# Two-layer decoder trunk on one core: merged router operations, another order at the entry of the expert loops, residual scaled tile by tile, down conversions in the last pass, last norm on three engines

## The reference

```python
h = layer_norm(ALPHA * h + mix, ln_g[layer, 0], ln_b[layer, 0])
ffn = grouped_moe(h, router_w, router_bias, moe_w_gate[layer], moe_w_up[layer], moe_w_down[layer])
h = layer_norm(ALPHA * h + ffn, ln_g[layer, 1], ln_b[layer, 1])

def grouped_moe(x, router_w, router_bias, w_gate, w_up, w_down):
    scores = jax.nn.softmax((xt @ router_w).astype(jnp.float32), axis=-1)
    ...      # best of 4 groups by the sum of its top 2, then the top 2 experts inside it
    h = jax.nn.silu(jnp.einsum('td,edf->tef', xt, w_gate)) * jnp.einsum('td,edf->tef', xt, w_up)
    h = h * gates[..., None].astype(h.dtype)
    y = jnp.einsum('tef,efd->td', h, w_down)
```

## Time and profile before

| what | us |
|---|---|
| median of 3 runs | 1335.28 |
| lowest and highest run | 1328.35 and 1341.85 |
| the profiled execution's own time | 1329.78 |
| its span, first to last instruction | 1328.1 |
| PE busy | 1180.5 (89%) |
| DVE busy | 909.9 (69%) |
| ACT busy | 685.1 (52%) |
| POOL busy | 184.9 (14%) |
| mean DMA rate | 213 GB/s |

### The profile page before, as it was taken

One profiled execution on the slowest core, in us unless ns is written; L12 is line 12 of the kernel. 1 busy time (PEld: TensorE's weight loads), 2 busy tenths in 40 slices (PEclk: granted clock), 3 DMA queues, 4 the chain that ended last, 5 costly groups with the idle time before them and its releaser, 6 DMA issues.

```text
span 1328.1 us, 14735 instructions
## 1 busy us (share of the span) xinstructions
PE 1180.5 (89%) x5648; PEld 943.1 (71%) x5649; DVE 909.9 (69%) x1299; ACT 685.1 (52%) x836; POOL 184.9 (14%) x141
## 2 busy tenths in 40 slices
PE   7998899947999999993899999999758999999970
PEld 5786478845888888872787766768747888888860
DVE  5243654766999999985524545665668999999854
ACT  4322334044777777764123544663147777777740
POOL 1000010111122212211101000001111122211112
PEclk9999999967999999997799999999768999999985
DMA  7131021074999999986113420411547999999933
GB/s 265 64 127 64 0 90 69 32 316 151 348 367 373 373 373 373 363 305 217 50 64 112 143 80 19 142 54 64 236 184 270 355 373 367 380 375 369 367 97 134
DMA packets 65450, 282.44 MB, mean 213 GB/s; under 512 B 11841, under 2 KB 12097, under 8 KB 40802
## 3 DMA queue, kind: packets, MB, share of 16 engines
q1 hardware_dynamic: 48672, 247.48, 49.2%
q0 software_dynamic: 12864, 29.42, 7.9%
q10 hardware_dynamic: 3842, 4.57, 1.0%
HBM read 270.91 MB, written 27.30 MB: 225 GB/s over the span
## 4 chain that ended last, share of the span: by engine, by line
PE 75%; DVE 12%; DMA 7%; ACT 3%; issue 2%; POOL 1%; POOLq 0%; SPq 0%; DVEq 0%; ACTq 0%
PE ps L657 21%; PE ps L659 20%; PE ps L658 20%; DVE ring_r L1387 4%; DMA ring<-in_moe_w_up_dram 4%; PE ps L998 2%; PE ps L704 2%; PE ps L1008 2%; PE ps L1021 1%; PE ps L768 1%; ACT ring_r L1154 1%; DMA ring<-in_gla_w_in_dram 1%; PE ps L774 1%; PE ps L651 1%; PE ps L759 1%
## 5 line engine op out<-in xcount | busy, mean ns | idle before, releaser
L1387 DVE TENSOR_TENSOR ring_r<-ring,ring_r 128x2048 fp32r<-128x2048 f32 x128 | 289.5, 2288 | 24.8 <-ACT ring_r L1154 24.8
L1154 ACT CAST ring_r<-ring 128x2048 fp32r<-128x2048 f32 x128 | 241.0, 1927 | 5.8 <-DMA ring<-in_moe_w_gate_dram 5.2
L658 PE MATMUL ps<-ring_r,xgT_r 128*128 128x512 f32 x512 | 202.4, 395 | 0.0
L1154 ACT CAST high_r<-ring 128x2048 fp32r<-128x2048 f32 x64 | 122.0, 1916 | 84.9 <-DMA ring<-in_moe_w_up_dram 83.4
L1387 DVE TENSOR_TENSOR ring_r<-ring,high_r 128x2048 fp32r<-128x2048 f32 x64 | 145.8, 2290 | 24.5 <-ACT high_r L1154 24.3
L552 POOL DMA_INDIRECT sum_rows<-arena,tokv x32 | 58.7, 1833 | 442.8 <-ACT arena L1195 429.8
L1381 DVE TENSOR_TENSOR ring_r<-ring,ring_r 128x1024 fp32r<-128x1024 f32 x72 | 84.2, 1221 | 41.9 <-ACT ring_r L1084 41.9
L658 PEld LDWEIGHTS ps<-ring_r,xgT_r 128*128 128x128 f32 x512 | 98.4, 192 | 18.7
L657 PE MATMUL ps<-ring_r,hidT_r 128*128 128x512 f32 x256 | 101.4, 396 | 10.9 <-DVE ring_r L1387 10.9
L657 PE MATMUL ps<-high_r,xgT_r 128*128 128x512 f32 x256 | 104.0, 406 | 4.9 <-DVE xgT_r L1592 4.9
L657 PE MATMUL ps<-ring_r,xgT_r 128*128 128x512 f32 x256 | 104.5, 408 | 0.0
(11 more groups left out here) (250 smaller groups left out, 2159.1 us busy)
## 6 DMA issues: line engine op xcount, KB each, us to landing
ring<-in_moe_w_gate_dram SPq DMA_DIRECT2D x64, 1024.0 KB, 10.0
ring<-in_moe_w_up_dram SPq DMA_DIRECT2D x64, 1024.0 KB, 11.5
ring<-in_moe_w_down_dram SPq DMA_DIRECT2D x64, 1024.0 KB, 10.3
ring<-in_gla_w_in_dram SPq DMA_DIRECT2D x6, 2048.0 KB, 8.1
ring<-in_kv_w_dram SPq DMA_DIRECT2D x4, 2048.0 KB, 9.5
ring<-in_fox_w_qg_dram SPq DMA_DIRECT2D x4, 2048.0 KB, 8.1
ring<-in_gla_w_out_dram SPq DMA_DIRECT2D x2, 2048.0 KB, 7.9
h_rows<-arena POOLq DMA_DIRECT2D x8, 512.0 KB, 5.9
```

Source lines behind the costliest of these rows:

```text
L658: pe.matmul(o, left[0], right[1], start=False, stop=False)
L1154: act.copy(high, w).then_inc(half_high, 1)
L1387: dve.tensor_tensor(low, w, high.bitcast(F32), ALU.subtract).then_inc(half_low, 1)
```

## The change

- `logits`: PE does the logits of tile s - 2 before the transposes of tile s - 1.
- Router on DVE: in `first_largest` the multiplication and the addition are one instruction (three calls), the mask of the group is added without the multiplication in front of it, the two fills of row numbers and the copy of the totals go to ACT, and `ranks` comes before the two gate columns. PE waits for `rt_info` too, and puts the totals in another PSUM bank.
- `take_normed`: ACT scales the residual of a tile right behind its transposed copy, instead of all four after the first weight casts.
- Entry of the loop: ACT casts halves 4 and 5 (gate of expert 1) before the stores to `sum_rows`, DVE subtracts them right behind `take_rows(0)`. `count_parts` moves behind turn 3.
- Loop: DVE makes the hidden values between the two gate halves of the next expert, no longer behind both.
- Last turn: PE transposes the hidden values of expert 15 before down(14). They go to a free piece of `xgT`. ACT and DVE convert the halves of down(15) around that, in turn 15.
- Last norm of layer 1: DVE subtracts the mean and multiplies by g, ACT multiplies by the inverse deviation, POOL adds b.

```diff
             def logits(L, s):
-                if 1 <= s <= T:
-                    pe.wait_ge(ln_ready, 2 * L * T + s)
-                    transpose_tile(TP_RT[L], s - 1, Hp)
                 if s >= 2:
                     pe.wait_ge(tp_dve, 2 * (4 * TP_RT[L] + s - 1))
                     mm = narrow(s - 2, rw)
                     if s == T + 1:
                         mm.then_inc(rt_logits, 1)
+                if 1 <= s <= T:
+                    pe.wait_ge(ln_ready, 2 * L * T + s)
+                    transpose_tile(TP_RT[L], s - 1, Hp)
...
+                    if e == E - 1:
+                        pe.wait_ge(ht_ev, E * L + e)
+                        pe.wait_ge(hid_done, E * L + e + 1)
+                        turn_hidden(hid).then_inc(ht_done, 1)
                     if e >= 1:
                         pe.wait_ge(ht_ev, E * L + e)
                         if e >= 2:
                             pe.wait_ge(y_ev, 2 * (E * L + e - 1))
                         down(e - 1)
-                    if e < E:
+                    if e < E - 1:
...
+            def shift(t):
+                pool.wait_ge(lnp_loaded, 64 * DEPTH)
+                pool.wait_ge(ln_scaled, t + 1)
+                pool.tensor_tensor(H[:, t, :], H[:, t, :], ln_p[:, 1, :], ALU.add).then_inc(ln_ready, 1)
...
+            def take_normed(L):
+                for t in range(T):
+                    take_tile(TP_RT[L], t)
+                    act.mul(dealt(H[:, t, :], K), blocks(Hp[:, t, :], K), ALPHA).then_inc(h_scaled, 1)
...
-                    do(dve.tensor_scalar(hit, hit, -float(n), None, ALU.mult))
-                    do(dve.tensor_tensor(key, hit, each_t(iota, n), ALU.add))
+                    do(dve.scalar_tensor_tensor(out=key, in0=hit, scalar=-float(n), in1=each_t(iota, n),
+                                                op0=ALU.mult, op1=ALU.add))
...
-                do(dve.tensor_tensor(four[4], four[3], in_group, ALU.mult))
-                do(dve.tensor_tensor(four[4], four[4], outside, ALU.add))
+                do(dve.tensor_tensor(four[4], four[3], outside, ALU.add))
...
-                own.mark(dve.tensor_copy(info[:, :, 0:E, 0], over_e(row_id[:, :])))
-                own.mark(dve.tensor_copy(info[:, :, 0:E, 1], over_e(row_id[:, :])))
...
+                if L == DEPTH - 1:
+                    for t in range(T):
+                        act.wait_ge(ln_centred, t + 1)
+                        act.wait_ge(ln_rstd, (2 * L + 1) * T + t + 1)
+                        act.mul(H[:, t, :], H[:, t, :], ln_r[:, t, 1:2]).then_inc(ln_scaled, 1)
```

More of the change, by code:

```diff
@@ L612, in experts @@
                     inverse_deviation(2 * L + 1, t)
+                    if L == DEPTH - 1 and t:
+                        shift(t - 1)
+                if L == DEPTH - 1:
+                    shift(T - 1)
             pool.wait_ge(sq_done, T * H_A)
@@ L1136, in tail @@
                 high_half(L, 1)
-                for t in range(T):
-                    take_tile(TP_RT[L], t)
+                take_normed(L)
             def router(L):
@@ L1142, in router @@
                 act.activation(rt[1], rt[0], ACT.Exp).then_inc(rt_exp, 1)
+                for m in range(2):
+                    act.copy(info[:, :, 0:E, m], row_id[:, :].unsqueeze(2).to_broadcast([P, T, E])
+                             ).then_inc(rt_info, 1)
+                act.wait_ge(rt_ranks, L + 1)
+                act.copy(total[:, :], ps[0:1, 5, 0:E]).then_inc(rt_total, 1)
             def high_half(L, n):
@@ L1186, in experts @@
                     if e + 1 < E:
-                        for kind in ("gate", "up"):
+                        for kind in ("gate", "up") if e >= 1 else ("up",):
                             high_half(L, half_of(kind, e + 1, 0))
                             high_half(L, half_of(kind, e + 1, 1))
+                    if e == E - 1:
+                        high_half(L, half_of("down", e, 0))
+                        take_hidden(e)
+                        high_half(L, half_of("down", e, 1))
                     if e >= 1:
@@ L1353, in _ @@
             high_half(1, 1)
-            for t in range(T):
-                take_tile(TP_RT[1], t)
+            take_normed(1)
             router(1)
@@ L1601, in experts @@
                         one_hots4(dve, 2, onehot[:, 0, :], hot, ranks, slot1)
-                    if e == 1:
-                        count_parts(L)
                 low_half(L, 2)
```

73 lines of the change are left out of this document (48 added, 25 removed).

## The result

The changed kernel took 1317.45 us in the median of 4 runs (1314.14 to 1323.07), the kernel before 1334.95 beside it. The ratio is 0.988, with a 95% interval of 0.985 to 0.992: 16 us (11 to 20) less. Six more runs of it beside the kernel before gave 0.986 (0.983 to 0.989). The forecast was 1307 us. In the profiled executions the span fell from 1328.1 to 1316.5, by 11.6, where the sum said 26.3. The kernel before was profiled in an execution 5.2 us under its median, so the traces show less than the runs. One of the 12 executions of the kernel of experiment 8 took 2647.24 us, twice the time of the others (1325.17 to 1333.18), and stands in no ratio.

What follows compares the result with a forecast made beforehand. PE was taken to bound the steady expert loop, DVE and weight stream close behind. Layer 0 -12.45, layer 1 -12.35 and norm -1.5 gave -26.3: 1303.5 from the profiled execution, 1309.0 from the median; 1307 written, range 1297 to 1324.

Steps and rivals of the forecast that it cites:

- Logits, +2.0 per layer: Router logits: doing tile 2's logits before tile 3's transposes costs 2.0 us per layer.
- The cover: In the old order, tile 2's logits hid ACT and DVE taking tile 3; the new order loses this.
- Router and entry, -6.5: Router operations and loop entry before the first weight halves: 3.6 us less in layer 0, 2.9 in layer 1.
- the first scatter is a whole turn away: Entry: the stores to `sum_rows`, issued some 9 us later, were expected to land well before the first scatter.
- First turn, -5.85 each: From expert 1's transposes to expert 2's: 14.15 us instead of 20.0, so 5.85 us less per layer.
- The rival that the stream takes it back: Weight stream returns both 5.85 us gains as waits in the last turns: 1315 us, by the median 1321; chance 0.15.
- Steady turns, "cost: nothing": Expert loop: making hidden values between DVE's two gate halves neither lengthens nor shortens a steady turn.
- Last turns, -11.1: Turns of experts 14 and 15: 5.5 us less in layer 0, 5.6 in layer 1, before +0.5 for loads.
- third rival: Last scatters collide or the clock falls, losing 9 of the last turns' 11 us: 1313, by the median 1318; chance 0.13.
- Last norm, -1.5: Layer 1's last norm split over DVE, ACT and POOL: 17.1 us instead of 18.6, so 1.5 us less.
- x = 1.84: Last norm: POOL's addition over 128x1024 put at two clears, 1.84 us, between bounds of 0.92 and 2.8.
- named signs of being wrong: Waits for weight halves or L1427, growing turn distance, last scatter long behind its copies, or POOL additions above 2.3 us.

Runs made afterwards that it cites:

- experiment 8: Kernel before with one edit on DVE: from expert 1 on, hidden values made between the next expert's two gate halves; 1328.15 us, ratio 0.997.
- experiment 7: Changed kernel with ACT issuing the four stores of the scaled residual behind the silu of expert 0; 1314.56 us, ratio 0.986 to the kernel before.
- experiment 5: Changed kernel with DVE making expert 15's hidden values between the two halves of down(14), not behind both; 1311.64 us, ratio 0.985 to the kernel before.
- experiment 6: Changed kernel with layer 0's second 2 MB mixer load behind the loads of the sums, its conversions behind the second tile; 1311.34 us, 0.984.

## Why the prediction was right or wrong, by its steps

- **The bound,** PE in the steady turn and gains only where it waits: right. The steady turns stayed at 18.15 us.
- **Logits, +2.0 per layer:** right, 2.3 in each. The cover that the prediction named as gone was gone.
- **Router and entry, -6.5:** measured -4.1, and -4.4 in the second profile. The router came as forecast: behind the logits DVE's first weight halves of the loop start 3.7 and 3.4 us earlier, for 3.6 and 2.9. Between them and the row transposes of expert 1 1.1 and 2.0 us were lost. The step that failed is "the first scatter is a whole turn away": the stores were not checked against the first gather, which they made 0.5 and 1.4 us longer (experiment 7 gives this back at the gather, and at the first turn in layer 1 alone). What the rest of the loss in layer 0 is stays open.
- **First turn, -5.85 each:** right, -5.75 and -6.1. The rival that the stream takes it back is true when the edit stands alone (4 of 11.6 us come back as slow turns), and false beside the gate order.
- **Steady turns, "cost: nothing":** nothing was lost, but a gain was overlooked. The kernel before already had slow turns at the end of each layer, 1.0 and 1.3 us over. The prediction read one steady turn at 352 and the landing times that grow to 14.3 us, and not the distance of the turns where they are longest. DVE held ready hidden values behind a half whose weights were late. The reordering takes most of it away: 0.1 to 1.8 us are left over both layers, and differ from one execution to the next.
- **Last turns, -11.1:** this is the step that failed most. Both halves of the third rival, "half of the ends is not had", came true. The table gives the change of three stretches in the two profiles of the changed kernel. The end of up(15) is the start of the hidden transposes less the wait before them, in the old order less the 5.45 us of down(14).

| stretch | forecast, layers 0 and 1 | layer 0 | layer 1 |
|---|---|---|---|
| row transposes of expert 15 to the end of up(15) | -0.8, -0.95 | -1.2 and -0.9 | 0.0 and +0.3 |
| end of up(15) to the first copy of down(15) | -4.7 each | -1.1 and -3.0 | -2.5 and -2.5 |
| that copy to the statistics | +0.5, 0 | +3.8 and +2.4 | +0.9 and +0.9 |

  In the first stretch the wait of 0.95 in layer 1 was said to go and stayed at 0.77 and 0.84: DVE came to the hidden values of expert 14 at 1249.88 only, some 5 us behind the end of up(14). In the second, the wait for the hidden values of expert 15 was put at 1.45 us and was 3.12 and 2.04, because the down halves of expert 14 stand before them on DVE (experiment 5: 1.38 without). In the old order down(14) had covered their making. The wait of 5.43 before down(15) did go: 1.21 is left, for 1.4 forecast. But the clock was not expected to fall there. In the first profile it fell in both layers and cost 1.4 and 1.6 us before the copy, in the second in layer 1 only. With both mended, in experiment 5, this stretch is 4.2 and 4.8 us shorter than before: the -4.7 was right but for these two terms. In the third, the scatter was put at 6.15 us with 0.5 for the two loads beside it, where it took 8.75 and pushed the next by 2.6 (experiment 6: 6.93 apart without). The row for 6.15 was of layer 1. Layer 0's own was 8.77.
- **Last norm, -1.5:** wrong in sign, +1.2. The choice of x = 1.84 us from two clears failed. It is 2.33. The Trainium skill, "GPSIMD Engine Reference", section 3.1, gave an estimated 2.25 and a term of zero, and the trace agrees with that price. But the larger miss is the end that was counted to. The span ends 6.6 us behind POOL's last operation, before as now. So the 17.1 us of the forecast had to be set against 17.2 to the last power (1321.46 - 1304.27), not against 18.6 to the last scaling on DVE. Even at x = 1.84 next to nothing was to be had, and the measured 18.36 less 17.19 is the 1.2. DVE's centring is held, which the prediction had not, but this cost nothing at the end, since POOL was never idle. It starts at 1298.77 inside POOL's addition (to 1299.92) and ends 1.1 us behind it. The Trainium skill, "SBUF — State Buffer", section "SBUF: two separate sides", says that a DVE operation with two inputs in SBUF and a GpSimd operation that reads SBUF take the same port pair one after the other. The trace fits that.

The time fell inside the range because the forecast leaned on the first turn, which came whole, because the range was wide, and because an overlooked gain of 2.4 us (1.2 in the second profile) stood against the losses at the ends. That is in part luck: the forecast 1307 lies below every run, and what came is the number of the third rival (by the median 1318), which had a chance of 0.13. Two of the named signs of being wrong also showed, a last scatter long behind its copies and POOL additions above 2.3 us.

## What to carry to other kernels

Before an edit in a loop that is fed at 99% of the DMA engines, list the distance of every turn, not one steady turn: where they grow, the order of an engine that mixes ready work with work on late data is worth more than the busy time says. When a wait is removed at the end of a loop, write down what it covered. And a transfer that is moved is to be checked against every other transfer that a later step waits for: gather and stores met here at the entry, scatter and load at the end. Last, before work is moved at the end of a program, look at what the end of the span waits for: here it followed POOL's last operation and not the last output.

## What the runs showed of the hardware

- **The clock behind a short wait of PE is not fixed by the wait.** From the transposes of expert 15's hidden values to the first copy of down(14) it takes 6.12 to 6.15 us when the products start 0.23 us apart, at full clock, and 7.5 to 7.8 when the first of them start 0.43 apart, at the lower one. With the new ends there are 16 such places. After waits of 1.36 to 1.38 us all 4 were quick. Of 9 after waits of 2.00 to 2.61, 4 were quick (the longest among them, 2.61) and 5 slow. After 3.03 to 3.21 all 3 were slow. The prediction had only the 1.64 of the earlier trace rows for it. The stretch of lower clock also differs after long idle times: the first products of layer 1's mixer reach full speed 13.4 us behind the first transposes in the kernel before and 15.6 in the changed one, 1.1 us of the ledger. That is no difference of the kernels: it is 14.7 us in the changed kernel's second profile and 13 to 16 over all profiles.
- **A plain load beside an indirect scatter that adds** stretched it from 5.94 us (experiment 6, 599.12 to its landing) to 8.75, and four stores of 512 KB ahead of a gather stretched this from 4.37 to 4.91 in layer 0 and 5.78 in layer 1, as measured to the first instruction that uses it.
- **An operation of DVE with two inputs in SBUF** took 2.26 instead of 1.28 us beside an addition on POOL.
- **The end of the program** came 6.61 us behind POOL's last operation in all 14 profiles, a power over 128x1 in the kernel before and an addition over 128x1024 in the changed one, with a drain on POOL for all but the last 0.2 of them. The last output had landed 2.6 and 4.0 us before the end.
